# Woven weight units: the low part of the next weights three rounds later, and gates stored before their sigmoid

## The reference

```python
# block 1: wide projection, three mixers, gated merge
proj = x @ w_in                                   # q, k, v, g of three branches; gate_logits_a, _b, _c
y_a = stick_breaking_attention(...) * silu(a_g)
y_b = head_rmsnorm(chunked_gated_linear_recurrence(h_q, h_key, h_i, log_f)) * silu(h_g)    # 4 heads of 64
y_c = head_rmsnorm(chunked_gated_linear_recurrence(c_q, c_k, c_v, c_log_f)) * silu(c_g)    # 4 heads, keys of 32
up = einsum("nbtw,nwd->nbtd", [y_a, y_b, y_c], w_up)
gates = sigmoid([gate_logits_a, gate_logits_b, gate_logits_c])
x = layer_norm(alpha * x + (gates * up).sum(0) @ w_out)
# block 2: rms_norm, projection, rwkv7_time_mix and mixed_dilated_attention (three patterns, 16 heads of 64), w_out
# block 3: rms_norm, projection, spatial gating and Fourier mix, w_out
```

## Time and profile before

| | us |
|---|---|
| runs | 3478.5, 3480.68, 3483.26 (median 3480.68) |
| profiled execution | 3486.47 |
| its span, first to last instruction | 3485.2 |
| TensorE matmul busy | 3096.1 |
| VectorE busy | 1945.3 |
| ScalarE busy | 1336.4 |
| mean granted TensorE clock | 0.952 |

### The profile page before, as it was taken

One profiled execution on the slowest core, in us unless ns is written; L12 is line 12 of the kernel. 1 busy time (PEld: TensorE's weight loads), 2 busy tenths in 40 slices (PEclk: granted clock), 3 DMA queues, 4 the chain that ended last, 5 costly groups with the idle time before them and its releaser, 6 DMA issues. The chain is left out here.

```text
span 3485.2 us, 66795 instructions
## 1 busy us (share of the span) xinstructions
PE 3096.1 (89%) x28304; PEld 2481.8 (71%) x28304; DVE 1945.3 (56%) x3481; ACT 1336.4 (38%) x2368; POOL 127.1 (4%) x132
## 2 busy tenths in 40 slices
PE   7997998899989988888866999969888899999998
PEld 5665676776667766666655887859887888777876
DVE  3555555523465256666675455446666666544465
ACT  3344344311244355555543444422322223453224
POOL 0000000000000111111110000000000000000000
PEclk9898999999999999999987999979999999999999
DMA  3000101142235411111111232351122115341114
GB/s 108 19 25 19 37 31 49 61 148 76 67 115 164 122 37 43 43 43 43 43 37 43 85 127 79 139 214 36 34 85 69 49 55 188 127 149 61 37 43 157
DMA packets 106089, 270.73 MB, mean 78 GB/s; under 512 B 8880, under 2 KB 49472, under 8 KB 104256
## 3 DMA queue, kind: packets, MB, share of 16 engines
q1 hardware_dynamic: 105792, 266.47, 23.0%
HBM read 209.81 MB, written 56.62 MB: 76 GB/s over the span
## 5 line engine op out<-in xcount | busy, mean ns | idle before, releaser
L196 PE MATMUL ps<-xs,wparts 128*128 128x512 f32 (+1 forms) x1664 | 703.1, 423 | 29.0 <-DVE wparts L264 28.0
L198 PE MATMUL ps<-xs,wparts 128*128 128x512 f32 (+1 forms) x1664 | 660.6, 397 | 0.0
L197 PE MATMUL ps<-xs,wparts 128*128 128x512 f32 (+1 forms) x1664 | 660.5, 397 | 0.0
L264 DVE TENSOR_TENSOR wparts<-wring,wparts 128x1024 fp32r<-128x1024 f32 x248 | 304.8, 1229 | 491.7 <-ACT wparts L256 469.8
L196 PEld LDWEIGHTS ps<-xs,wparts 128*128 128x128 f32 (+1 forms) x1664 | 318.6, 191 | 132.5 <-issue 61.0
L256 ACT ACTIVATE wparts<-wring 128x1024 fp32r<-128x1024 f32 x248 | 262.8, 1060 | 306.0 <-PE ps L198 213.8
L198 PEld LDWEIGHTS ps<-xs,wparts 128*128 128x128 f32 (+1 forms) x1664 | 317.4, 191 | 73.1 <-issue 0.6
L197 PEld LDWEIGHTS ps<-xs,wparts 128*128 128x128 f32 (+1 forms) x1664 | 319.1, 192 | 61.5 <-issue 4.8
L2049 ACT ACTIVATE Pm<-Pm,ml 128x128 f32<-128x128 f32 (+1 forms) x384 | 167.7, 439 | 188.5 <-DVE ml L2114 188.1
L2114 DVE CUSTOM_DVE_ANT_0 Pm<-ps,mask 128x128 f32<-128x128 f32 (+1 forms) x384 | 110.4, 347 | 114.1 <-PE ps L1957 113.8
L2410 ACT ACTIVATE M<-ps 128x256 f32<-128x256 f32 x160 | 61.5, 384 | 257.2 <-PE ps L2221 248.6
(11 more groups left out here) (399 smaller groups left out, 5894.3 us busy)
## 6 DMA issues: line engine op xcount, KB each, us to landing
wring<-in_wo SPq DMA_DIRECT2D x96, 512.0 KB, 3.7
ops<-rw SPq DMA_DIRECT2D x32, 640.0 KB, 5.6
wring<-in_w SPq DMA_DIRECT2D x39, 512.0 KB, 3.7
wring<-in_w2u SPq DMA_DIRECT2D x33, 512.0 KB, 3.9
wring<-in_wg SPq DMA_DIRECT2D x24, 512.0 KB, 3.9
wring<-in_w2v SPq DMA_DIRECT2D x24, 512.0 KB, 4.3
wring<-in_w2a SPq DMA_DIRECT2D x24, 512.0 KB, 4.8
Vc<-vr SPq DMA_DIRECT2D x32, 256.0 KB, 3.4
```

What stands on the lines that cost most here:

```text
L196: nc.tensor.matmul(out, a, c, start=start, stop=False)
L197: nc.tensor.matmul(out, b, c, start=False, stop=False)
L198: return nc.tensor.matmul(out, a, d, start=False, stop=stop)
L264: K.nc.vector.tensor_tensor(W.part(i, 1), W.raw(i), W.part(i, 0).bitcast(F32), ALU.subtract).then_inc(*K.dve.done("w_lo", W.first + i))
```

## The change

Two things are done. In the woven units (`unit_dve`, `hgrn_units_dve`, `prep_units_dve`) `w_lo` of the next unit moves from round 0 to round 3 on VectorE, while `w_hi` stays in round 0 on ScalarE; the number of rounds of a unit stays eight. And the twelve early gates are evicted with a plain copy and stored raw. In the merge, ScalarE waits for the stored gate, takes the sigmoid of the whole tile in place (`back_act`, between `w_hi` and the evictions of its unit), and VectorE waits for that in place of the transfer.

```diff
--- before.py
+++ after.py
@@ -51,6 +51,7 @@
     "out_norm": "o3g o3a o3v o3i o3y",
     "out_norm_act": "o3sq o3r",
     "merging": "gated merge",
+    "gates": "sig kept",
     "between": "state st_own",
     "recurrence": "g kn st o y",
     "stick_pe": "s t av",
@@ -304,11 +305,13 @@
     yield STEP
 
 
-def unit_dve(K, W, i, pauses=7):
+def unit_dve(K, W, i):
+
+    for _ in range(3):
+        yield STEP
     yield from w_lo(K, W, i + 1)
-    for _ in range(pauses):
-        yield STEP
-    yield STEP
+    for _ in range(5):
+        yield STEP
 
 
 GROUPS = [(0, 1, 2), (3, 4, 5), (6, 7)]
@@ -599,7 +602,7 @@
 
 def gate_store(K, A, B, j):
 
-    K.sp.wait_ge(*(yield "sig", j, 1))
+    K.sp.wait_ge(*(yield "kept", j, 1))
     K.nc.sync.dma_start(A["gt"][j], B.kept[j % 3]).then_inc(*K.sp.done("gate_store", j, slot=j % 3, by=16))
 
 
@@ -1026,18 +1029,20 @@
     nc.scalar.activation(X, X, ACT.Exp, scale=-1.0).then_inc(*act.done("dexp", ri, lev))
 
 
-def gate_act(K, B, j, dst, ready):
+def gate_act(K, B, j, dst, ready, name="sig", func=ACT.Sigmoid, more=()):
     nc, act, u = K.nc, K.act, gate_unit(j)
     yield from w_hi(K, B.W, u + 1)
-    for _ in range(5):
+    yield STEP
+    yield from more
+    for _ in range(4):
         yield STEP
     for h in range(2):
         act.wait_ge(*(yield "u", u, h))
         if ready:
             act.wait_ge(*(yield ready[h]))
         act.in_order()
-        nc.scalar.activation(dst[:, half(h)], K.bank["u", u, h], ACT.Sigmoid).then_inc(
-            *act.done("sig", j, h, also=[("sig_u", u, h)]))
+        nc.scalar.activation(dst[:, half(h)], K.bank["u", u, h], func).then_inc(
+            *act.done(name, j, h, also=[("sig_u", u, h)]))
         for s in range(0 if h else 2):
             yield STEP
     yield STEP
@@ -1045,13 +1050,21 @@
 
 def gates_act(K, B, js):
     for j in js:
-        yield from gate_act(K, B, j, B.kept[j % 3], [("gate_store", j - 3)] * 2 if j >= 3 else [])
+        yield from gate_act(K, B, j, B.kept[j % 3], [("gate_store", j - 3)] * 2 if j >= 3 else [], "kept", ACT.Copy)
+
+
+def back_act(K, B, j):
+
+    K.act.wait_ge(*(yield "gate_back", j))
+    K.act.in_order()
+    K.nc.scalar.activation(B.back[j % 2], B.back[j % 2], ACT.Sigmoid).then_inc(*K.act.done("sig", j))
 
 
 def merge_act(K, B):
     for j in range(EARLY, 24):
         yield from gate_act(K, B, j, B.E, [("merge", j - 1, h) for h in range(2)] if j >= 17 else
-                            [("gated", j - 1, h) for h in range(2)] if j > EARLY else [])
+                            [("gated", j - 1, h) for h in range(2)] if j > EARLY else [],
+                            more=back_act(K, B, j - EARLY))
 
 
 def b1_act(K, A, B):
@@ -1136,8 +1149,10 @@
 def hgrn_units_dve(K, B, p):
     nc, dve, u = K.nc, K.dve, 8 + 4 * p
     q, kk, lf, v = B.hg_set[p]
+    for _ in range(3):
+        yield STEP
     yield from w_lo(K, B.W, u + 1)
-    for _ in range(7):
+    for _ in range(4):
         yield STEP
     dve.wait_ge(*(yield "f_sig", u, 1))
     dve.in_order()
@@ -1356,7 +1371,7 @@
             yield STEP
         if n == EARLY - 1:
             yield from m_lo(K, B, OUT_K[0])
-        yield from branch_dve(K, B, n, B.back[n % 2], [("gate_back", n)] * 2)
+        yield from branch_dve(K, B, n, B.back[n % 2], [("sig", n)] * 2)
         yield from branch_dve(K, B, j, B.E, [("sig", j, h) for h in range(2)])
         yield STEP
 
```

## The result

The changed kernel takes 3431.64 us (median; 3428.93 to 3440.66) against 3480.48 us (four runs of the kernel before), a ratio of 0.9867 with a 95% interval of 0.9854 to 0.9879. The forecast was 3436 us. The profiled execution took 3428.97 us.

A forecast was written before the change was run, and what follows sets the result against it. TensorE (busy 89%) bounds; only its gaps ending on VectorE or ScalarE work behind the low part can give. 25.5 + 4.2 + 16.2 = 45.9 us off 3486.5; on the median's scale 3434.8, stated as 3436, range 3415 to 3465.

The forecast's parts named there:

- Third recurrence: Levels 21.1 us, opening gap 3.4 us and clock 1 us: 25.5 us to be gained in this stage.
- the low part ahead of the third copy in two levels: In two of the recurrence's six levels, the low part's new place was to cost 0.9 us each.
- A floor read from a gapless half: Two gapless halves of 5.41 us make 10.82 us a level, against 14.94 us; six levels' floor 24.7 us lower.
- First two recurrences: Three places where TensorE waits for a chain behind the low part: 1.3, 1.3 and 1.56 us, sum 4.2 us.
- Attention: The 2.86 us stop at the low part leaves VectorE's chain: 2.7 us in each of six groups, 16.2 us.
- the rival in which the clock comes back: Over the attention groups, shorter gaps bring 17 us of TensorE's clock back, time 3418 us; chance 0.13.
- Preparation and margins: No gain where TensorE has no gap; low part early enough, 3.2 us to spare, tightest at the first recurrence's start.
- The rival that the low part comes too late: In the preparation, TensorE waits 6.1 us in each of seven groups, 43 us; time 3500 us; chance 0.05.
- The load behind it ... Cost zero: On SyncE's queue, weight loads and what is queued behind them issue up to three rounds later, at zero cost.
- if the merge units grow: Sign at the merge: longer units there would show the prediction wrong; no size was given.
- Raw gates: Table loads go; 12 added sigmoids, 12.7 us of ScalarE, lie beside merge units and were taken to cost nothing.
- Well under 200 us: Sign at line 264, the low part: its waits fall from 470 us to well under 200.

## Why the prediction was right, and where not

The total came within 4.4 us, with three terms off, and two of them, the first recurrences and the merge, hid part of the third, the attention. That the sum is so close is in part luck.

**Third recurrence** (25.5 forecast, 25.8 found). The levels gave 89.63 - 69.14 = 20.5 us against 21.1, and the opening 4.85 us (22.35 to 17.50 from the first scores to those of the first level) against 3.4 and a share of the clock. Waits of 0.7 to 1.1 us remain, 3.7 us in four places, against 3.6 allowed. That they are the low part ahead of the third copy in two levels is not borne out: with the low part in round 6 the idle time of the levels falls from 3.9 to 2.9 us only. What the sum did not say is its make-up. A floor read from a gapless half at full clock contains the clock, and 9.3 of the 25.9 us are that. The experiments divide the gain between the parts: 20.6 by the move, 5.2 more by the raw gates.

**First two recurrences** (4.2 forecast, 3.1 found; 2.8 from the start of the span). The two waits behind a low part fell by 1.3 us each (11.25 to 9.92 and 6.66 to 5.33), and the gap of 1.56 us closed, which are the three terms of the forecast. A fourth place, not looked at, took 1.3 us back: at the end of the first recurrence the low part now stands between two copies that line 1289 and with it TensorE wait for, and the wait of 0.98 us there became 2.30.

```profile
382.85 1.23 DVE L265 TENSOR_TENSOR wparts<-wring,wparts 128x1024 fp32r<-128x1024 f32 x1
...
388.58 0.66 PE L753 MATMUL ps<-cc,h 128*128 128x128 f32 x4 [2.30 <-DVE h L1293]
```

**Attention** (16.2 forecast, 21.6 to 23.5 found). The mechanism was right, and so was the count of waits that matter. The size of the term was off: a group is 3.9 us shorter, not 2.7. Of that 2.1 are idle time, near the forecast, and 1.8 are clock. This is the rival in which the clock comes back, true in part: it was given 17 us, and 9.0 us came in five groups. The reason against it, that the large gap stays, was right as to the gap (6.35 to 7.0 us at once) and wrong as to the clock. The chain was misread as well: the prediction followed it to line 2162, whose gap gained nothing.

**Preparation and margins.** Nothing forecast, 0.0 found. At the second unit of a group the low part ends at 1961.24 and TensorE starts on it at 1964.43: 3.2 us, as worked out. At the start of the first recurrence it ends at 313.47, and TensorE starts at 313.97: 0.5 us.

```profile
1960.01 1.23 DVE L265 TENSOR_TENSOR wparts<-wring,wparts 128x1024 fp32r<-128x1024 f32 x1
...
1964.43 0.39 PE L197 MATMUL ps<-xs,wparts 128*128 128x512 f32 x1
...
312.24 1.23 DVE L265 TENSOR_TENSOR wparts<-wring,wparts 128x1024 fp32r<-128x1024 f32 x1
...
313.97 0.39 PE L197 MATMUL ps<-xs,wparts 128*128 128x512 f32 x1
```

The rival that the low part comes too late named the right place; with round 6 its price was 20.5 us, not 43.

**"The load behind it ... Cost zero".** This step failed. It asked whether the weight load itself was late, and that one is not. It did not follow the queue to what stands behind: weight load 37 takes the slot that the low part of unit 35 read, and that low part, in round 3, ended at 686.64, 1.3 us after the last input that x's reload waits for (line 1340, 685.30). The gate's store stands between them, so the reload was issued at 687.51, 2.2 us after its last input. With it the `up` loads behind came later against the work, and TensorE waited 3.09 us where it had waited 1.1. The forecast was zero, and it is 2.0 us. By the prediction's own sign (wrong "if the merge units grow") this part of it is wrong. With the low part back in round 0 the wait is gone, and so it is with the loads issued ahead.

**Raw gates.** The added sigmoids cost nothing on the path, as taken, though the first one waits 11.40 us for its transfer. "Well under 200 us" of waits at line 264 was wrong: 301.5 us are left. And one table load is left at the opening's exponential.

**The drain, and the engine to start at.** The drain that the Trainium skill (ScalarE: Activation LUTs, section What ACT_TABLE_LOAD costs) adds to a load does not show in the changed kernel either: at 539.51 the load takes 1.28 us, and the exponential starts at 540.80. The rule of the Trainium skill to start at the engine with the highest occupancy (Perfetto Trace Analysis, section Identifying the Most-Contended Engine) names TensorE here, and the 1.3% came from TensorE's own gaps and clock, with none of its work taken away. So the prediction's reading, that by this rule the time would stay, was too strong.

## What to carry to other kernels

Where engines run in order, put an operation that is needed late behind the work that is ready and wanted soon, and place it by the tightest stage: here one round was enough for the attention, the recurrence wanted three, and six were too many for the preparation. Idle time in front of an operation is worth nothing by itself: 63.5 us of it went in the preparation and brought no time. When an operation moves, follow every queue that waits for it to what is queued behind, not only to the transfer that it frees. And read length minus busy and busy at equal count apart, in two windows cut at the same instructions: the first is waits, the second is clock where the granted clock moves with it. It does not always: in the five attention groups of round 6 TensorE was busy for 358.2 us at a granted clock of 0.97, in the changed kernel for 354.4 us at 0.95, and no run here shows why.

## What the hardware showed beyond that

TensorE's clock moved with the small gaps. In the third recurrence the granted clock was 0.93 with 23.55 us idle in 178.80, 0.96 with 17.03 idle (raw gates alone), 0.97 with round 1 (13.5 idle), 0.99 with 10.1 (the move alone) and 1.00 with 6.94. A share of 1.00 is 2.4 GHz, and 0.50 is 1.2 GHz. Over the five kernels each us of idle time removed took about half a us of busy time with it. In the attention this is not so orderly: 0.94 with 69.4 us idle, 0.92 with 63.7, 0.95 with 62.4 or 59.0, and 0.97 with 55.7 (round 6).
